# Second feed-forward opening: low halves by block, additions ahead of squares; half of the activation store signalled apart

## The reference

```python
def _rms_norm(v, g):
    r = lax.rsqrt(jnp.mean(vf * vf, axis=-1, keepdims=True) + EPS)
    return (vf * r).astype(v.dtype) * g

def _swiglu(u, w_gate, w_up, w_down):
    return (jax.nn.silu(u @ w_gate) * (u @ w_up)) @ w_down
...
h = h + 0.5 * _swiglu(_rms_norm(h, ffn1_norm[l]), ffn1_w_gate[l], ffn1_w_up[l], ffn1_w_down[l])
...
h = h + 0.5 * _swiglu(_rms_norm(h, ffn2_norm[l]), ffn2_w_gate[l], ffn2_w_up[l], ffn2_w_down[l])
```

## Time and profile before

| | us |
|---|---|
| median of 3 runs | 2134.73 (2132.18 to 2135.2) |
| profiled execution | 2131.39 |
| its span | 2129.6 |
| PE busy in the span | 2051.5 (96%) |
| DVE, POOL, ACT busy | 1417.6, 1225.0, 639.1 |

### The profile page before, as it was taken

One profiled execution on the slowest core, in us unless ns is written; L12 is line 12 of the kernel. 1 busy time (PEld: TensorE's weight loads), 2 busy tenths in 40 slices (PEclk: granted clock), 3 DMA queues, 4 the chain that ended last, 5 costly groups with the idle time before them and its releaser, 6 DMA issues.

```text
span 2129.6 us, 24461 instructions
## 1 busy us (share of the span) xinstructions
PE 2051.5 (96%) x9194; PEld 1678.2 (79%) x9194; DVE 1417.6 (67%) x1602; ACT 639.1 (30%) x979; POOL 1225.0 (58%) x802
## 2 busy tenths in 40 slices
PE   8899999999999999999999999899999999999996
PEld 4787778788878787888887888787788888887885
DVE  6677677566866979763334355447676777787778
ACT  5423322223434510001121223225222323244452
POOL 6389687778545443222333431036699998985551
PEclk9999999999999999999999999999999999999998
DMA  7422432346777454332113142211123223267763
GB/s 266 144 96 95 147 117 94 104 141 257 251 267 252 149 169 89 98 102 62 50 50 119 50 160 63 104 42 49 69 92 128 94 92 112 94 227 269 262 222 133
DMA packets 140628, 286.37 MB, mean 134 GB/s; under 512 B 12384, under 2 KB 37600, under 8 KB 140128
## 3 DMA queue, kind: packets, MB, share of 16 engines
q1 hardware_dynamic: 100496, 233.21, 32.3%
q10 hardware_dynamic: 40016, 51.61, 7.5%
HBM read 222.39 MB, written 63.42 MB: 134 GB/s over the span
## 4 chain that ended last, share of the span: by engine, by line
PE 65%; DVE 20%; DMA 5%; POOL 4%; issue 3%; ACT 2%; SPq 1%; DVEq 0%; ACTq 0%; POOLq 0%
PE ps L524 64%; DMA raw<-in_dn 3%; DVE w_lo L2350 3%; DVE xt_lo L2340 2%; DVE f_g L1787 2%; DVE h L2359 2%; POOL w_lo L1114 1%; DMA d_act<-f_g 1%; DVE acc L1787 1%; POOL start_room L1210 1%; POOL raw L1142 1%; DVE sq L2153 1%; POOL raw L1193 1%; DVE ua_lo L1796 1%; DVE ua_lo L1787 1%
## 5 line engine op out<-in xcount | busy, mean ns | idle before, releaser
L1114 POOL TENSOR_TENSOR w_lo<-raw,w_hi 128x512 fp32r<-128x512 f32 x352 | 552.8, 1586 | 219.7 <-ACT w_hi L1349 219.4
L524 PE MATMUL ps<-xt_hi,w_hi 128*128 128x512 f32 x1320 | 517.7, 392 | 10.2 <-DVE xt_lo L2340 9.0
L524 PE MATMUL ps<-xt_hi,w_lo 128*128 128x512 f32 x1320 | 514.1, 389 | 0.0
L524 PE MATMUL ps<-xt_lo,w_hi 128*128 128x512 f32 x1320 | 514.0, 389 | 0.0
L1349 ACT ACTIVATE w_hi<-raw 128x512 fp32r<-128x512 f32 x462 | 279.2, 627 | 517.0 <-POOL raw L1142 262.9
L1122 POOL TENSOR_SCALAR w_hi<-raw 128x1024 fp32r<-128x1024 f32 x54 | 62.9, 1164 | 476.6 <-PE ps L524 469.2
L524 PEld LDWEIGHTS ps<-xt_hi,w_hi 128*128 128x128 f32 x1320 | 248.3, 188 | 70.4 <-issue 15.6
L524 PEld LDWEIGHTS ps<-xt_hi,w_lo 128*128 128x128 f32 x1320 | 248.0, 188 | 52.1
L524 PEld LDWEIGHTS ps<-xt_lo,w_hi 128*128 128x128 f32 x1320 | 248.3, 188 | 50.9
L1142 POOL TENSOR_TENSOR raw<-raw 128x512 f32<-128x512 f32 x178 | 272.9, 1543 | 12.8 <-DMA raw<-in_gu 5.5
L1193 POOL TENSOR_TENSOR raw<-raw 128x512 f32<-128x512 f32 x110 | 166.9, 1527 | 140.8 <-DMA raw<-in_dn 140.8
(11 more groups left out here) (310 smaller groups left out, 2890.8 us busy)
## 6 DMA issues: line engine op xcount, KB each, us to landing
raw<-in_dn SPq DMA_DIRECT2D x264, 256.0 KB, 3.5
raw<-in_gu SPq DMA_DIRECT2D x88, 512.0 KB, 5.6
raw<-in_weights SPq DMA_DIRECT2D x54, 512.0 KB, 3.5
d_act<-acc SPq DMA_DIRECT2D x20, 512.0 KB, 2.8
d_act<-sq SPq DMA_DIRECT2D x20, 512.0 KB, 3.8
d_act<-f_g SPq DMA_DIRECT2D x20, 512.0 KB, 4.6
h<-in_x SPq DMA_DIRECT2D x16, 512.0 KB, 8.9
xt_hi<-d_act SPq DMA_DIRECT2D x8, 1024.0 KB, 7.6
```

The lines of the kernel that those rows point to most:

```text
L524: ins = nc.tensor.matmul(out, lhsT, rhs, start=start, stop=stop)
L1114: add(lo, src, hi.bitcast(F32), op=ALU.subtract).then_inc(s_w_low["pool"], 1)
```

## The change

In the second feed-forward's opening `x_low` writes the low parts of one block at a time: blocks 0 and 1 of each depth block first, then block 2 of all four. PE takes `w11` and `w12` over the four depth blocks and then `s4` over the four. DVE does its first four additions of step 0 ahead of the last two additions of squares. The sums of squares stand two ops later in PE's order, and ACT's root stands ahead of the copy into `acc`. In both feed-forwards k = 2 of `act_sum` gives a signal of its own, SP stores the two parts in `f_g` after it and `acc` and `sq` after k = 4, and even steps wait for the first pair, odd steps for the second.

```diff
-SUMS_AT, SPREAD_AT = (1, 1), (1, 6)
+SUMS_AT, SPREAD_AT = (1, 3), (1, 6)
...
@@ PE, step 0 @@
                     wait_b_low(kp)
                     for op in first[4:6]:
                         first_pass(op, kp)
-                    for k in ((), (0, 1), (2,), (3,))[kp]:
-                        first_pass(first[6], k)
+                for kp in range(KP):
+                    if f:
+                        pe.wait_ge(s_xb_lo, 2 * (KP - 1) + 2 * KP + kp + 1)
+                    first_pass(first[6], kp)
...
@@ SP, act_store @@
+                sp.wait_ge(s_act_g, (FP - 1) * f + p + 1)
+                sp.dma_start(d_act[1:4:2, p].rearrange("c p x -> p c x"), two(f_g[:, 0])).then_inc(s_gstore, 16)
+                sp.dma_start(d_act[6, p], f_g[:, 1, 0:HALF]).then_inc(s_gstore, 16)
                 sp.wait_ge(s_act, FP * f + p + 1)
-                for x, to in ((two(acc[:]), d_act[0:3:2, p]), (two(sq[:]), d_act[4:6, p]), (two(f_g[:, 0]), d_act[1:4:2, p])):
+                for x, to in ((two(acc[:]), d_act[0:3:2, p]), (two(sq[:]), d_act[4:6, p])):
                     sp.dma_start(to.rearrange("c p x -> p c x"), x).then_inc(s_actst, 16)
-                sp.dma_start(d_act[6, p], f_g[:, 1, 0:HALF]).then_inc(s_actst, 16)
...
@@ ACT, steps @@
                                 if f == 1:
+                                    root()
                                     act.wait_ge(s_norm, 5)
...
-                                act.wait_ge(s_actst, 64 * ((FP - 1) * f + n // 2))
+                                act.wait_ge(s_actst if n % 2 else s_gstore, 32 * ((FP - 1) * f + n // 2))
                             copy(F[0][:, C0], n, 0)
-                        if f == 1 and n == 1 and i == 1:
-                            root()
...
@@ ACT, first_acts @@
                         act.wait_ge(s_gstep, last + i)
+                        act.wait_ge(s_gstore, 32 * (FP - 1) * (f + 1))
...
@@ DVE, opening_raw @@
-                def x_low(k):
-                    for j in range(2):
-                        m = 2 * k + j
...
+                def x_low(k, b):
+
+                    m, at = 2 * k + (b > 0), C1 if b == 2 else C0
+                    dve.wait_ge(s_xb_hi, 2 * (KP * f + k) + (b > 0) + 1)
+                    v.scalar_tensor_tensor(out=xb_lo[:, b, k], in0=h[:, m, at], scalar=gains[:, gi, m:m + 1],
+                                           in1=xb_hi[:, b, k].bitcast(F32), op0=ALU.mult, op1=ALU.subtract).then_inc(s_xb_lo, 1)
...
                     for k in range(KP):
-                        x_low(k)
+                        x_low(k, 0)
+                        x_low(k, 1)
+                    for k in range(KP):
+                        x_low(k, 2)
...
@@ DVE, step 0 @@
-                if f:
-                    add_squares(KT - 2)
-                    add_squares(KT - 1)
                 copied(0, 1)
                 op_done(0, 3)
                 add(F[1][:, C0], q["s3"], F[0][:, C1])
                 add(F[1][:, C1], q["s1"], F[1][:, C0])
                 add(F[1][:, C0], q["w22"], F[1][:, C0])
                 add(F[0][:, C1], q["s1"], F[0][:, C1])
+                if f:
+                    add_squares(KT - 2)
+                    add_squares(KT - 1)
...
@@ DVE, act_sum @@
-                    tt(acts_at(len(DN) - 1, FP - 1) if last else f_g[:, 1, C0], y[:, C0], y[:, C1], ALU.add)
+                if k == 2 and last:
+                    tt(acts_at(len(DN) - 1, FP - 1), y[:, C0], y[:, C1], ALU.add)
+                elif k == 2:
+                    v.tensor_tensor(f_g[:, 1, C0], y[:, C0], y[:, C1], ALU.add).then_inc(s_act_g, 1)
```

More of the change, by code:

```diff
@@ L356, in build @@
         s_diag, s_spread, s_rn = sem("diag_written"), sem("norm_spread"), sem("norm_kept")
-        s_gcopy, s_gadd, s_gate, s_silu, s_act, s_actst = (sem(n) for n in
-            ("gu_bank_copied", "gu_bank_added", "gate_scaled", "silu_written", "act_written", "act_stored"))
+        s_gcopy, s_gadd, s_gate, s_silu, s_act, s_actst, s_act_g, s_gstore = (sem(n) for n in
+            ("gu_bank_copied", "gu_bank_added", "gate_scaled", "silu_written", "act_written", "act_stored",
+             "act_in_gate_written", "act_in_gate_stored"))
         s_acts = [[sem(f"acts_loaded{b}_{c}") for c in range(len(ACT_CHUNKS))] for b in range(4)]
@@ L661, in wait_b_low @@
                     else:
-                        pe.wait_ge(s_xb_lo, 2 * (kp if f == 0 else kp + 4))
+                        pe.wait_ge(s_xb_lo, 2 * (kp if f == 0 else kp + KP))
                 first = [next(passes) for _ in range(7)]
@@ L988, in act_store @@
             def act_store(f, p):
+                two = lambda t: t.rearrange("p (c x) -> p c x", c=2)
+                sp.wait_ge(s_act_g, (FP - 1) * f + p + 1)
+                sp.dma_start(d_act[1:4:2, p].rearrange("c p x -> p c x"), two(f_g[:, 0])).then_inc(s_gstore, 16)
+                sp.dma_start(d_act[6, p], f_g[:, 1, 0:HALF]).then_inc(s_gstore, 16)
                 sp.wait_ge(s_act, FP * f + p + 1)
-                two = lambda t: t.rearrange("p (c x) -> p c x", c=2)
-                for x, to in ((two(acc[:]), d_act[0:3:2, p]), (two(sq[:]), d_act[4:6, p]), (two(f_g[:, 0]), d_act[1:4:2, p])):
+                for x, to in ((two(acc[:]), d_act[0:3:2, p]), (two(sq[:]), d_act[4:6, p])):
                     sp.dma_start(to.rearrange("c p x -> p c x"), x).then_inc(s_actst, 16)
-                sp.dma_start(d_act[6, p], f_g[:, 1, 0:HALF]).then_inc(s_actst, 16)
             def act_load(f, s, c):
@@ L2074, in add_squares @@
                         dve.wait_ge(s_sqadd, m)
-                def x_low(k):
-                    for j in range(2):
-                        m = 2 * k + j
-                        dve.wait_ge(s_xb_hi, 2 * (KP * f + k) + j + 1)
-                        if j == 0:
-                            out, x, hi = xb_lo[:, 0, k], h[:, m, C0], xb_hi[:, 0, k]
-                        else:
-                            out, x, hi = xb_lo[:, 1:3, k], two(h[:, m]), xb_hi[:, 1:3, k]
-                        v.scalar_tensor_tensor(out=out, in0=x, scalar=gains[:, gi, m:m + 1], in1=hi.bitcast(F32),
-                                               op0=ALU.mult, op1=ALU.subtract).then_inc(s_xb_lo, 1)
+                def x_low(k, b):
[3 more added lines that the diff above has]
+                                           in1=xb_hi[:, b, k].bitcast(F32), op0=ALU.mult, op1=ALU.subtract).then_inc(s_xb_lo, 1)
                 def b_low(k):
@@ L2330, in act_sum @@
                     tt(f_g[:, 0, C1], x[:, C0], y[:, C1], ALU.add)
-                if k == 2:
-                    tt(acts_at(len(DN) - 1, FP - 1) if last else f_g[:, 1, C0], y[:, C0], y[:, C1], ALU.add)
+                if k == 2 and last:
+                    tt(acts_at(len(DN) - 1, FP - 1), y[:, C0], y[:, C1], ALU.add)
+                elif k == 2:
+                    v.tensor_tensor(f_g[:, 1, C0], y[:, C0], y[:, C1], ALU.add).then_inc(s_act_g, 1)
                 if k == 3:
```

## The result

The changed kernel takes **2107.5 us** (median of 4 runs, 2105.8 to 2113.9) against 2135.0 us for the kernel before beside it: ratio 0.988, 95% interval 0.9855 to 0.9903. The profiled execution took 2109.0 us, 22.4 less than the profiled one of before.

The account below looks back on a forecast made before the run. The prediction took the kernel as bound by PE, busy 96% of the span. Its terms summed to -15.4 us from the profiled 2131.4, giving 2116.0; with 3.3 us for the runs' higher median it forecast 2119.3 us, range 2112 to 2128.

Parts of the forecast that it names:

- Site 1: First table turn, first feed-forward (175.53 us): copy wait goes, DVE is late next; -0.7 us (0.7 to 4.7).
- Site 2: Turn 44 us later: waits for copy and addition go, with the half-clock stretch; -3.4 us (1.7 to 3.4).
- Table waits: PE's waits at products turning tables into filter kernels, first feed-forward steps 10 and 14; the prediction had no term.
- Low parts of the opening: Second feed-forward's opening: twelve smaller low-part instructions instead of eight, estimated between 1.5 us sooner and 1.4 later; 0 us.
- Sums: Sums of squares, second feed-forward's opening: PE's 1.72 us wait and half clock behind go; -5.3 us (1.7 to 5.7).
- signs of being wrong: PE waiting for `w_lo` in steps 1 to 3 or at the spread, `xb_lo` at 1.7 us throughout, new half-clock stretches.
- Store of the second feed-forward: First store there: of PE's 3.7 us wait 0.6 stays, the half-clock stretch goes; -4.8 us (1.5 to 5.4).
- `w_lo`: POOL's `w_lo`, late by 1.2 us twice together after the store held ACT, comes in time; -1.2 us (0 to 1.5).
- pace the opening: Rival: twelve low parts take 1.67 us each, two more stretches run at half clock; 2127.4 us, chance 0.12.
- the gain wasn't absorbed: Rival: PE comes earlier but waits longer for independent work, about a tenth of the gain stays; 2133 us, chance 0.08.
- the collisions of DVE and POOL: Rival: with ACT held shorter, POOL works beside DVE and collides on chains PE waits for; 2140.3 us, chance 0.06.

Follow-up runs that it names:

- e4: e1 with SP waiting for the end of the whole step's sums before issuing the first store, order and semaphores kept: 2117.5 us, ratio 0.9934.
- e1: Kernel before with only the stores' part (k = 2 signal, split stores, separate waits) in both feed-forwards: 2110.8 us, ratio 0.9904.
- e5: Changed kernel with the low parts in pairs and `s4` interleaved, as before the change: 2106.7 us, ratio 0.9904 to the kernel before.
- e2: Kernel before with only the opening's part (low parts, additions, sums, root) changed, stores as before: 2125.9 us, ratio 0.9983.
- e3: Kernel before with the stores' part in the first feed-forward only, the second storing and waiting as before: 2118.2 us, ratio 0.995.
- e7: Changed kernel with ACT's root back behind the copy: 2111.1 us, ratio 0.9923 to the kernel before.
- e6: Changed kernel with the sums of squares two passes earlier, additions still ahead of the squares: 2112.4 us, ratio 0.9935 to the kernel before.
- e11: e1 with ACT's copies in even and odd steps waiting for both groups of stores: 2122.8 us, ratio 0.9973 to the kernel before.

## Why the prediction was wrong

Term by term, from the second profiled execution of the changed kernel in the table:

- Site 1, -0.7: **-4.0**, the step that failed first. The reasoning was right that DVE's table work is late next, and e4 shows it. But its end was taken from the rows of before as if fixed. It moved: with ACT freed sooner POOL works and stands at other moments, and those operations take about half the time when they begin while POOL stands. The changed kernel in both executions, e1 and e5 all have the pair at 2.47 us, and e4, which differs from e1 in the signal alone, at 4.55. The prediction's upper end of 4.7 had it; the choice of the low end, "as DVE's own rows are nearest", was the mistake.
- Site 2, -3.4: -3.9.
- Table waits, no term: **-2.5**. The list of waits had 8.6 us for them, and I left the line out as untouched by the change. Their price hung on DVE operations beside POOL, like site 1's; that is read from the rows below, and no run tested it apart. In the changed kernel, right ahead of the product (POOL ends at 289.63 by these rows, whose times on POOL are rough, and then stands for over 4 us):

```profile
289.08 1.02 DVE L1805 COPY tables<-rn 64x256 f32<-64x256 f32 x2
290.13 1.22 DVE L1793 TENSOR_TENSOR tables<-tables 128x1024 f32<-128x1024 f32 x1
```
```profile
287.92 1.71 POOL L1120 TENSOR_TENSOR w_lo<-raw,w_hi 128x512 fp32r<-128x512 f32 x1
```

  and in the kernel before, where POOL works through:

```profile
295.56 1.97 DVE L1799 COPY tables<-rn 64x256 f32<-64x256 f32 x2
297.56 2.24 DVE L1787 TENSOR_TENSOR tables<-tables 128x1024 f32<-128x1024 f32 x1
```
```profile
296.07 1.31 POOL L1114 TENSOR_TENSOR w_lo<-raw,w_hi 128x512 fp32r<-128x512 f32 x1
297.45 1.26 POOL L1142 TENSOR_TENSOR raw<-raw 128x512 f32<-128x512 f32 x1
```

  The product waits for the copy, which takes 1.02 us instead of 1.97.

- Low parts of the opening, 0: -0.3. Twelve took 14.8 us, within the 13.8 to 16.7 of the two ways it was worked out. Five waits of 0.4 to 0.7 us came, not two of 1 to 1.5. The stretch at half clock at 1470.4 went too, which the prediction didn't count, and the longer row of low parts took it back (e5).
- Sums, -5.3: -5.1. Neither a wait nor half clock is left. At the spread a wait of 0.4 us came, one of the signs of being wrong, and over the whole spread 1.0 us went back, for which there was no term. From the sums' result to the diagonal DVE and ACT took 8.6 us (1475.87 to 1484.46), just over the 8.2 us that the prediction said would hide them, and 6.1 us in the kernel before.
- Store of the second feed-forward, -4.8: -3.8 beside the opening, -5.1 alone (e1). The copy started at 1510.60, k = 2 had ended at 1506.99: 3.6 us, as forecast; the wait is 0.4 us. But 9 us behind it stands the new wait of 0.7 us for `w_lo` in step 3, which the prediction had named as a sign of being wrong; in e1 it is 0.2 us.

```profile
1510.60 0.60 ACT L1448 ACTIVATE f_g<-ps 128x512 f32<-128x512 f32 x1 [12.56 <-DMA d_act<-f_g]
```
```profile
1506.30 0.69 DVE L2339 TENSOR_TENSOR f_g<-sq 128x512 f32<-128x512 f32 x1
```

- `w_lo`, -1.2: -1.9 up to 1890 us, and +0.4 behind it. The two waits went, but not for the reason given. ACT had been held by the store ahead of each, yet they are gone in e2 and e3 too, where the second feed-forward stores as before and the shift moves there by -1.5 and -1.4. What decides them stays open, so this term came out by luck.

The sum is -20.1 instead of -15.4. The other 7 us of the miss are no step of the mechanism. The prediction added 3.3 us because the profiled execution of before was below its median; that of after was 1.5 above its own. And the profiled pair differs by 2.3 more than the places explain: it won 2.8 us between 540 and 1455 us and 0.6 more behind 1545, and had lost 1.2 ahead of 160, all where the change has no part or the shift moves in every kernel. On four other chips the kernel before had medians of 2127 to 2129 us, not 2135, and on the one where the changed kernel ran again its gain was 18 us (15 to 21). The range lacked a term for what comes and goes from one execution to the next (3.7 us sooner to 2.9 later from 400 to 1455 us alone), which is in none of its steps. The terms by themselves, -20.1 us, would have given 2114.6, inside the range; below it the time fell by this part.

The rivals: the low parts didn't pace the opening, the gain wasn't absorbed, and the collisions of DVE and POOL, put down as a way to be slower, were the unforeseen gain. The Trainium skill (SBUF — State Buffer, section SBUF: two separate sides) says that a loser of the shared port "fully blocks". The rows of 2.47 against 4.5 us agree, about 1.0 us more for each of the two with POOL at work; no run here shows the port itself. That rule has two signs, and I used one.

## What to carry to other kernels

When an edit frees an engine sooner, don't take the durations behind it from the old trace as fixed: ask which operations there have a short and a long duration, and whether the edit moves what they collide with. Price every wait in PE's list that hangs on such operations, even at places that the change leaves alone. Read gains by the shift of matched instructions at each place; with stretches at half clock that come and go, a median of a few runs may not show a loss of 4 us, as in e7.

## What the runs showed of the hardware

- The same DVE operation, two of 1024 elements with both inputs in SBUF, took 2.47 us for the pair with POOL standing and 4.5 with POOL at work, and the third took 1.22 in e4 and 2.20 elsewhere. No run took POOL's work away by itself; the link is that in the changed kernel, e1, e4 and e5 the short duration begins where POOL stands.
- The lower clock level (0.50) came with waits of PE of 2.1 us and more at site 1 in e4, at the sums in e6 and at the spread in e7, and went with them. The length of a wait doesn't decide it by itself. The wait of 2.43 us at the store in e11 has the clock at 1.00 behind it, and so have waits of 3.2 and 2.7 us in the attention of the changed kernel, behind each of which the kernel before had 3.4 us at half. And in the changed kernel 3.4 us at half begin at 851.1 us, where the last wait, of 0.7 us, had ended at 848.2.
- At site 1, at the sums and at the store in e1 the gain was about the wait removed and 1.7 us more for each 3.4 us at half that went (4.0, 5.1 and 5.1 us). At the low parts a stretch of 3.4 us at half went and only 0.3 us was gained.
- Splitting DVE's low parts of 1024 elements into halves cost little: 14.8 us for twelve against 13.8 for eight.
